# Attention with its values held stationary, and eight modulation chunks moved to the second layer's rotation and scan

## The chip, the cores and the metric

The kernel is one program on one core of a Trainium2 chip. The metric is the device time of one execution in microseconds, as a median over runs. All data is float32 except two small masks in the expert routing.

## What is computed

Two layers of a diffusion transformer over 512 tokens (256 context, 256 latent) of width 1024. Of each layer, cut to what matters here:

```python
def diff_attend(q, k, v, lam):            # 4 heads, two maps per head, 32 wide each
    s = jnp.einsum('bqhmd,bkhmd->bhmqk', q, k).astype(jnp.float32) * (DA_QK ** -0.5)
    p = jax.nn.softmax(s, axis=-1)
    a = p[:, :, 0] - lam * p[:, :, 1]
    return jnp.einsum('bhqk,bkhv->bqhv', a.astype(v.dtype), v)

for i in range(DEPTH):
    mod_x = jnp.split((c_act @ w_mod[i] + b_mod[i])[:, None, :], 6, axis=-1)   # mod_c likewise
    u = concat(ada_norm(hc, g, mod_c[0], mod_c[1]), ada_norm(hx, g, mod_x[0], mod_x[1]))
    proj = u @ w_in[i]
    o_da  = rms_norm(diff attention, subln_g) * (1.0 - lam_init)   # per head of 64 values
    o_ssd = ssd_mixer(...)                                         # a scan in chunks, both directions
    o_mla = mla_attend(...)                                        # 4 heads, 96 wide, values 64 wide
    mix = concat(o_da, o_ssd, o_mla) @ w_out[i]
    hx = hx + mod_x[2] * mix                                       # hc likewise
    hx = hx + mod_x[5] * moe_ffn(ada_norm(hx, g2, mod_x[3], mod_x[4]))   # 16 experts, top 2
return rms_norm(hx, final_norm_g)
```

Context queries see the 256 context keys, latent queries all 512. In the second layer only the latent tokens are queries.

## The kernel before

The program is written engine by engine; each engine executes its list in order and the lists meet at semaphores. A layer runs input projections, latent norms, the start and states of the scan, `rotate` (rotary embedding of queries and keys), `scan_tiles`, `attention`, `out_projection`, the router, and the experts, whose weights (about 100 MB a layer) are streamed by the SP queue.

**Attention.** A unit is one head of one kind on one tile of 128 queries. `attention_units` lists, for each tile, four "da" units (differential, two maps) and then four "ml" units: 32 units in the first layer (16 against 256 keys, then 16 against 512) and 16 units in the second (all against 512). Step s of every engine handles stages of several units:

- TensorE: scores of unit s (L737 for da, two matmuls; L740 for ml, one), transposes of the probabilities of unit s-2 (`tr`, L446), probabilities times values of unit s-3 (L770: the transposed probabilities are the stationary operand, 64 value columns the moving one).
- VectorE: maximum of the scores of unit s (L1344) and its scaling (L1345), then for unit s-1 the reciprocal of the sums and, for da, the scaling of map 1 and its subtraction (L1353 to L1356). Per group of four heads it takes the result out, squares and sums it, normalises it and places it (L1373 to L1398), with transposes by TensorE between.
- ScalarE: exponentials with row sums of unit s (L1832), copy of the transposed probabilities of unit s-2 (L1843).

Score banks alternate 2,3 and 4,5 of PSUM; the scores of unit s wait until the exponentials of unit s-2 are done.

**Modulation.** Each layer's `c @ w_mod` is 3 groups of four chunks. A chunk is a 2 MB load into one of four ring slots and one part of `spare`: 8 matmuls with tiny weights (L468). A fifth part per group transposes the row (L446, after a copy by VectorE, L1057) and places it (L1061). `spare(n)` does the next n parts wherever it is called: 5 in the first norm, 5 in `rotate` of the first layer, 7 in its `scan_tiles`, and 13 in its attention, one in each of steps 2 to 14. Then all 30 parts are done, so the calls in the second layer do nothing. SP loads the ring's chunks in the order of the list `chunks`, then writes zeros to the expert slots (25 MB), then starts on the experts; a slot is loaded again when its last reader is done.

GpSimd (POOL) works in the scan (L2028 to L2053) and is idle in the attention of before.

Of the kernel before, what the change touches and what calls it, by code (L numbers as in the profile page):

```python
# [8 lines left out]
ALU = mybir.AluOpType  # L9
# [51 lines left out]
SCAN_MODS = (1, 1, 1)  # L61
ROUTER_BANK = 5
MODS_LEFT = 13
# [3 lines left out]
LAG_OUT, LAG_NORM, LAG_TURN, LAG_PLACE = 7, 8, 9, 10  # L67
# [99 lines left out]
def head_part(s, lag):  # L167

    g, rest = divmod(s - lag, DA_H)
    return g if rest == 0 and g >= 0 else None  # L170
# [21 lines left out]
def hybrid_dit_kernel(nc, consts, x, c, ctx, c_ctx, norm_mix_g, norm_ffn_g, w_mod, b_mod, w_in, w_out, da_lambda,  # L192
# [3 lines left out]
    with ExitStack() as stack:  # L196
# [81 lines left out]
        probs_t = take(1024, tmp_at + 3072).rearrange("p (b k q) -> p b k q", b=2, q=P)  # L278
        stats = take(4 * 64, tmp_at + 4096).rearrange("p (s u m) -> p s u m", s=4, m=2)
        o_sb = take(512, tmp_at + 4352).rearrange("p (k n) -> p k n", n=256)  # L280
        o_sq = take(256, tmp_at + 4864)
# [99 lines left out]
        def turned_probs(n, nk):  # L381

            return ps[:, 6 if nk == NCTX else 6 + n % 2, :]

# [38 lines left out]
        def _(pe):  # L423
# [227 lines left out]
            def scan_tiles(l):  # L651
# [22 lines left out]
                for d in range(2):  # L674
                    cast_rows(0, d)
                    spare(SCAN_MODS[0])
                scores(1)
                cast_rows(1, 0)
                for i, t in enumerate(tiles):
# [17 lines left out]
                    if i + 1 < len(tiles):  # L697
                        cast_rows(i + 1, 1)
                        spare(SCAN_MODS[1])
                    if i + 2 < len(tiles):  # L700
                        scores(i + 2)
                        cast_rows(i + 2, 0)
                        spare(SCAN_MODS[2])
# [10 lines left out]
            def attention(l):  # L714
                units = attention_units(l)
                before, groups_before = units0 * l, units0 // DA_H * l
                pe.wait_ge(S("roped"), l + 1)
                for s in range(len(units) - DA_H + LAG_TURN + 1):
# [9 lines left out]
                    if s < len(units):  # L728
# [3 lines left out]
                        pair = 2 + 2 * (s % 2)  # L732
                        if kind == "da":
                            r0 = 64 * (hh % 2)
                            for m in range(2):
                                r = slice(r0 + 32 * m, r0 + 32 * m + 32)
                                last = nc.tensor.matmul(ps[:, pair + m, 0:nk], qk[r, hh // 2, P * t:P * t + P],  # L737
                                                        qk[r, 2 + hh // 2, 0:nk], start=True, stop=True)
                        else:
                            last = nc.tensor.matmul(ps[:, pair, 0:nk], qm[0:HD, hh, P * t:P * t + P],  # L740
# [4 lines left out]
                    if 0 <= n < len(units):  # L745
                        kind, t, hh, nk = units[n]
                        if kind == "da":
                            pe.wait_ge(S("mixed"), before // 2 + sum(1 for x in units[:n + 1] if x[0] == "da"))
                        else:
                            pe.wait_ge(S("exp_done"), before + n + 1)  # L750
                        if n >= 1 and units[n - 1][3] == NCTX:
                            pe.wait_ge(S("probs_t_ready"), before + n)
                            if nk > NCTX:
                                pe.wait_ge(S("mod_placed"), DEPTH * DEPTH_GROUPS)
# [5 lines left out]
                    n = s - 3  # L760
                    if 0 <= n < len(units):
                        kind, t, hh, nk = units[n]
                        g = n // DA_H
                        if hh == 0 and g >= 2:

                            pe.wait_ge(S("o_placed"), groups_before + g - 1)
# [7 lines left out]
                    g = head_part(s, LAG_TURN)  # L774
                    if g is not None:
                        pe.wait_ge(S("o_ready"), groups_before + g + 1)
                        for m in range(2):
                            last = tr(ps[:, g % 2, 256 + P * m:256 + P * m + P],
# [1455 lines left out]
```

## Time and profile before

| what | us |
|---|---|
| median of three runs (1418.46 to 1428.31) | 1423.97 |
| span of the profiled execution | 1417.9 |
| TensorE busy in it | 1172.4 (83%) |
| VectorE busy | 463.5 (33%) |
| ScalarE busy | 266.9 (19%) |
| GpSimd busy | 122.1 (9%) |

The span is that of one execution. In the chain of work that ended last, TensorE has 61% of the span, DMA 20%, VectorE 11% and ScalarE 3%. A float32 matmul stands as two records in the views, a transpose as one.

### The profile page before, as it was taken

How to read it: one execution, taken by the hardware profiler on the slowest of the kernel's cores; microseconds unless marked ns; L12 is line 12 of the kernel's file. 1: busy time of each engine (PE TensorE's matmuls, PEld its weight loads, DVE VectorE, ACT ScalarE, POOL GpSimd, SP SyncE). 2: the span in 40 equal slices, each digit the busy share in tenths (PEclk: the TensorE clock that was granted, in tenths of full speed). 3: DMA queues.
4: the chain of work that ended last, by engine and by line, in shares of the span. 5: the costliest groups of instructions: out<-in, count | busy, mean ns of one | idle time of the engine just before them, and what ended most of it. 6: DMA issues, size and time to landing. Idle time of an engine off the chain costs nothing.

```text
span 1417.9 us, 15930 instructions
## 1 busy us (share of the span) xinstructions
PE 1172.4 (83%) x6032; PEld 567.1 (40%) x6032; DVE 463.5 (33%) x1121; ACT 266.9 (19%) x592; POOL 122.1 (9%) x107
## 2 busy tenths in 40 slices
PE   5899978878989599999985499986799699995553
PEld 2363433444654333333332447432468333332222
DVE  5111456764742611111101421357663511110003
ACT  1220101223530411111101322001251311110002
POOL 2000031820000010000000200033200100000001
PEclk9999999979899799999998699997689799997776
DMA  9622106739996389999999401006003689999972
GB/s 337 242 86 93 60 0 261 289 131 412 374 353 274 140 326 372 389 390 395 395 399 397 187 4 56 0 0 237 0 1 119 252 313 385 388 410 413 407 327 93
DMA packets 86997, 344.03 MB, mean 243 GB/s; under 512 B 6918, under 2 KB 42187, under 8 KB 64395
## 3 DMA queue, kind: packets, MB, share of 16 engines
q1 hardware_dynamic: 67728, 309.68, 56.5%
q10 hardware_dynamic: 15195, 19.86, 4.1%
q0 software_dynamic: 4000, 13.49, 2.7%
q8 instruction: 48, 0.79, 0.2%
q14 instruction: 26, 0.21, 0.0%
HBM read 300.92 MB, written 42.07 MB: 242 GB/s over the span
## 4 chain that ended last, share of the span: by engine, by line
PE 61%; DMA 20%; DVE 11%; ACT 3%; issue 2%; SPq 1%; POOL 1%; ACTq 0%; POOLq 0%; DVEq 0%
PE ps L901 13%; PE ps L503 12%; DMA ring<-in_exp_w_up 10%; PE ps L924 6%; PE ps L791 6%; PE ps L512 5%; PE ps L446 4%; DMA ring<-in_w_mod 3%; DMA slots<-arena 2%; PE ps L468 2%; DMA arena<-in_exp_w_up 2%; PE ps L688 2%; PE ps L770 2%; PE ps L668 2%; PE ps L740 1%
## 5 line engine op out<-in xcount | busy, mean ns | idle before, releaser
L901 PE MATMUL ps<-ring,arena 128*32 128x256 f32 (+1 forms) x1344 | 197.8, 534 | 45.1 <-DMA ring<-in_exp_w_up 45.1
L503 PE MATMUL ps<-u,ring 128*128 128x512 f32 (+1 forms) x416 | 168.0, 564 | 9.5 <-ACT u L1743 4.0
L446 PE MATMUL ps<-cst,arena 128*128 128x128 f32 x558 | 110.3, 318 | 65.7 <-DVE arena L1445 33.0
L446 PEld LDWEIGHTS ps<-cst,arena 128*128 128x128 f32 x558 | 70.2, 160 | 172.0 <-issue 81.5
L901 PEld LDWEIGHTS ps<-ring,arena 128*32 128x32 f32 (+1 forms) x1344 | 71.3, 136 | 154.4 <-issue 146.5
L1601 DVE TENSOR_TENSOR arena<-arena,ps 128x128 f32<-128x128 f32 (+1 forms) x59 | 27.3, 503 | 317.3 <-ACT arena L1903 317.3
L503 PEld LDWEIGHTS ps<-u,ring 128*128 128x128 f32 x416 | 80.0, 194 | 94.9 <-issue 90.1
L901 PE MATMUL ps<-arena 128*64 128x512 f32 (+1 forms) x544 | 82.2, 528 | 17.6 <-DMA arena<-in_exp_w_up 17.6
L924 PE MATMUL ps<-arena 128*32 128x256 f32 (+1 forms) x672 | 94.4, 485 | 1.6 <-ACT arena L1912 1.6
L791 PE MATMUL ps<-u,ring 128*128 128x512 f32 (+1 forms) x256 | 83.6, 487 | 2.3 <-DVE h L1426 1.3
L512 PE MATMUL ps<-ring,u 128*128 128x256 f32 (+1 forms) x224 | 76.6, 502 | 7.7 <-DVE arena L1245 7.7
L1611 DVE COPY arena<-ps 128x512 f32<-128x512 f32 (+1 forms) x44 | 26.4, 601 | 161.6 <-DMA slots<-arena 85.7
L1903 ACT ACTIVATE arena<-ps 128x256 f32<-128x256 f32 (+1 forms) x44 | 15.3, 348 | 331.6 <-PE ps L901 302.8
L791 PEld LDWEIGHTS ps<-u,ring 128*128 128x128 f32 x256 | 48.3, 190 | 35.9 <-issue 29.7
L512 PEld LDWEIGHTS ps<-ring,u 128*128 128x128 f32 x224 | 44.3, 200 | 37.6 <-issue 34.3
L468 PE MATMUL ps<-ring,cond 128*32 128x512 f32 x384 | 52.1, 670 | 8.3 <-DMA ring<-in_w_mod 6.7
L2012 POOL DMA_INDIRECT arena<-slots,slot_ids x12 | 12.1, 1008 | 541.1 <-ACTq L1945 538.1
L1832 ACT ACTIVATE arena<-ps,arena 128x512 f32<-128x512 f32 (+1 forms) x72 | 43.9, 614 | 64.3 <-DVE arena L1345 61.8
L901 PEld LDWEIGHTS ps<-arena 128*64 128x64 f32 (+1 forms) x544 | 29.2, 133 | 63.2 <-issue 59.8
L1344 DVE TENSOR_REDUCE arena<-ps 128x2 f32<-128x1024 f32 (+3 forms) x48 | 39.5, 822 | 36.3 <-PE ps L740 29.4
L924 PEld LDWEIGHTS ps<-arena 128*32 128x32 f32 (+1 forms) x672 | 31.9, 122 | 46.5 <-issue 41.2
L770 PE MATMUL ps<-arena 128*128 128x64 f32 x320 | 46.7, 291 | 1.9 <-ACT arena L1843 1.9
(291 smaller groups left out, 1221.9 us busy)
## 6 DMA issues: line engine op xcount, KB each, us to landing
ring<-in_w_mod SPq DMA_DIRECT2D x24, 2048.0 KB, 10.9
ring<-in_exp_w_gate SPq DMA_DIRECT2D x22, 2048.0 KB, 18.6
ring<-in_exp_w_up SPq DMA_DIRECT2D x22, 2048.0 KB, 23.0
arena<-in_exp_w_down SPq DMA_DIRECT2D x22, 2048.0 KB, 20.1
slots<-zeros SPq DMA_DIRECT2D x4, 6144.0 KB, 41.9
arena<-in_exp_w_gate SPq DMA_DIRECT2D x10, 2048.0 KB, 20.7
u<-in_exp_w_down SPq DMA_DIRECT2D x10, 2048.0 KB, 19.7
arena<-in_exp_w_up SPq DMA_DIRECT2D x10, 2048.0 KB, 26.7
```

The costliest lines, as they stand in the source:

```text
L446: return nc.tensor.transpose(dst, src, ident[0:n, 0:n])
L468: last = nc.tensor.matmul(bank[32 * j:32 * j + 32, :], cond[:, k, :], w[:, k2, 512 * j:512 * j + 512], start=(k == 0), stop=(k == 7), tile ...
L503: last = nc.tensor.matmul(bank[row:row + width, 0:T - c0], w[:, k, n:n + width], u[:, k, c0:T], start=(k == 0), stop=(k == KT - 1))
L512: last = nc.tensor.matmul(bank[:, i * width:(i + 1) * width], u[:, k, P * t:P * t + P], w[:, k, n:n + width], start=(k == 0), stop=(k == K ...
L668: last = nc.tensor.matmul(ps[:, 2 + b, :], ones[:, :], ews[i % 2][d][:, 4 * b:4 * b + 4, :].rearrange("p h i -> p (h i)"), start=True, sto ...
L688: last = nc.tensor.matmul(ps[:, 4, 64 * hh:64 * hh + 64], ews[i % 2][d][:, hh, :], xdt_of(i, d)[:, 64 * hh:64 * hh + 64], start=(d == 0 an ...
L770: last = nc.tensor.matmul(ps[:, g % 2, 64 * hh:64 * hh + 64], probs_t[:, n % 2, k, :], v[:, k, 64 * hh:64 * hh + 64], start=(k == 0), stop ...
L791: last = nc.tensor.matmul(bank[:, 0:T - c0], w[:, k, P * m:P * m + P], u[:, k, c0:T], start=(k == 0), stop=(k == KT - 1))
L901: last = nc.tensor.matmul(ps[n * part:n * part + n, 2 + b % 2, 0:2 * width].rearrange("p (s n) -> p s n", s=2), x_k, pair[:, :, a:a + widt ...
L924: last = nc.tensor.matmul(ps[n * part:n * part + n, 6 + b % 2, 0:width], hid_t[:, f % 2, n * (f // 2):n * (f // 2) + n], w[:, f, width * p ...
L1344: link(v.tensor_reduce(mx[:, s, 0:nm], ps[:, pair:pair + nm, 0:nk], AX.X, ALU.max))
L1832: last = a(probs[:, s % 3, m, 0:nk], ps[:, 2 + 2 * (s % 2) + m, 0:nk], ACT.Exp, scale=DA_SCALE if kind == "da" else MLA_SCALE, bias=nb[:, ...
```

## The change

The units of a tile alternate da and ml. Each kind has score banks of its own (da 2 and 3, ml 4). The score scales go into the queries when they are copied out of PSUM, so the maximum is written negated at once and the exponential needs no scale. The ml probabilities are divided by their sum before the transposes, by GpSimd. The values become the stationary operand and the transposed probabilities (128 columns) the moving one; two heads run side by side in the columns of the array, once per two units of a kind. The result comes out with features on partitions, so it needs no transposes; the mean of squares over a head is a matmul with a block matrix of ones. The chunks of groups 1 and 2 of the second layer are loaded after its input projection chunks, and their ten parts run in its `rotate` (5) and `scan_tiles` (2, 2 and 1); the first layer's attention keeps 3 parts.

```diff
-SCAN_MODS = (1, 1, 1)
+SCAN_MODS = ((1, 1, 1), (2, 1, 0))
-MODS_LEFT = 13
+MODS_LEFT = 3
+MODS_FIRST = 20
-LAG_OUT, LAG_NORM, LAG_TURN, LAG_PLACE = 7, 8, 9, 10
+HEAD_UNITS = 2 * DA_H
+LAG_PV, LAG_SQUARE, LAG_MEAN, LAG_ROOT, LAG_ML, LAG_DA = 3, 10, 10, 11, 11, 12
...
-            for t in range(0 if layer == 0 else NCTX // P, TT) for kind in ("da", "ml") for hh in range(DA_H)]
+            for t in range(0 if layer == 0 else NCTX // P, TT) for hh in range(DA_H) for kind in ("da", "ml")]
...
-        chunks += [("mod", 1, g, k) for g in range(3) for k in range(4)]
+        chunks += [("mod", 1, 0, k) for k in range(4)]
         chunks += [("out", 0, n, 0) for n in range(2)]
-        after = [("in", 1, n, 0) for n in ("x", "bcv", "dtm", "qk", "z")] + [("out", 1, n, 0) for n in range(2)]
+        after = [("in", 1, n, 0) for n in ("x", "bcv", "dtm", "qk", "z")]
+        after += [("mod", 1, g, k) for g in (1, 2) for k in range(4)]
+        after += [("out", 1, n, 0) for n in range(2)]
```

In TensorE's attention:

```diff
-                            pe.wait_ge(S("exp_done"), before + n + 1)
+                            pe.wait_ge(S("ml_scaled"), (before + n) // 2 + 1)
...
-                        for k in range(nk // P):
-                            last = nc.tensor.matmul(ps[:, g % 2, 64 * hh:64 * hh + 64], probs_t[:, n % 2, k, :],
-                                                    v[:, k, 64 * hh:64 * hh + 64], start=(k == 0),
-                                                    stop=(k == nk // P - 1))
+                    if 0 <= n < len(units) and n % 4 >= 2:
+                        for k in range(nk // P):
+                            for unit in (n - 2, n):
+                                hh = units[unit][2]
+                                r, c = 64 * (hh % 2), P * (hh // 2)
+                                last = nc.tensor.matmul(heads_of(kind)[r:r + 64, c:c + P],
+                                                        v[:, k, 64 * hh:64 * hh + 64], probs_t[:, unit % 4, k, :],
+                                                        start=(k == 0), stop=(k == nk // P - 1),
+                                                        tile_position=(0, r))
...
+                    i = tile_part(l, s, LAG_MEAN)
+                    if i is not None:
+                        pe.wait_ge(S("o_squared"), units0 // HEAD_UNITS * l + i + 1)
+                        nc.tensor.matmul(ps[:, 5, 0:256], head_ones, o_sq, start=True,
+                                         stop=True).then_inc(S("o_means"), 1)
```

In VectorE's attention:

```diff
-                        link(v.tensor_reduce(mx[:, s, 0:nm], ps[:, pair:pair + nm, 0:nk], AX.X, ALU.max))
-                        ts(nb[:, s, 0:nm], mx[:, s, 0:nm], -(DA_SCALE if kind == "da" else MLA_SCALE), None,
-                           ALU.mult).then_inc(S("max_ready"), 1)
+                        v.tensor_reduce(nb[:, s, 0:nm], scores_of(kind)[:, :, 0:nk], AX.X, ALU.max,
+                                        negate=True).then_inc(S("max_ready"), 1)
...
-                            link(v.reciprocal(rr[:, n, 0:1], rs[:, n, 0:1]))
+                            v.reciprocal(rr[:, n, 0:1], rs[:, n, 0:1]).then_inc(S("mixed"), 1)
...
+                if kind == "da":
+                    dve.wait_ge(S("o_root"), tiles_back + i + 1)
+                    placed = stt(u[:, 0:2, P * t:P * t + P], heads, vec[:, l, V_SUBG:V_SUBG + 1],
+                                 o_root.rearrange("p (m n) -> p m n", n=P), ALU.mult, ALU.mult)
...
+                    placed = v.tensor_copy(u[:, 6:8, P * t:P * t + P], heads)
```

In ScalarE's attention:

```diff
+                        a(o_sq, heads_of("da"), ACT.Square).then_inc(S("o_squared"), 1)
+                        rsqrt(o_root, ps[:, 5, 0:256], S("o_root"), 1.0 / (DA_V * keep), small[:, 21 + l:22 + l])
```

In GpSimd's list, between the scan and the experts:

```diff
+            def attention(l):
+                for n, (kind, _, _, nk) in enumerate(attention_units(l)):
+                    if kind == "ml":
+                        pool.wait_ge(S("mixed"), units0 * l + n + 1)
+                        part = probs[:, n % 3, 0, 0:nk]
+                        g.tensor_scalar(part, part, rr[:, n, 0:1], None, ALU.mult).then_inc(S("ml_scaled"), 1)
```

TensorE in the attention of the first layer, third tile of queries, before. L737 and L740 are the scores of da and ml units, L446 with x4 the transposes of one unit's probabilities, L446 with x2 those of a group's result, L770 the product with the values of one unit.

```order
L740 MATMUL ps<-arena 128x512
L446 MATMUL ps<-cst,arena 128x128 x4
L770 MATMUL ps<-arena 128x64 x4
L737 MATMUL ps<-arena 128x512 x2
L446 MATMUL ps<-cst,arena 128x128 x4
L770 MATMUL ps<-arena 128x64 x4
L737 MATMUL ps<-arena 128x512 x2
```

The same place after the change (L759 and L762 are the scores, L469 the transposes, L795 the product with the values of two units).

```order
L762 MATMUL ps<-arena 128x512
L469 MATMUL ps<-cst,arena 128x128 x4
L795 MATMUL ps<-arena 64x128 x8
L759 MATMUL ps<-arena 128x512 x2
L469 MATMUL ps<-cst,arena 128x128 x4
L795 MATMUL ps<-arena 64x128 x8
L762 MATMUL ps<-arena 128x512
L469 MATMUL ps<-cst,arena 128x128 x4
L759 MATMUL ps<-arena 128x512 x2
L469 MATMUL ps<-cst,arena 128x128 x4
```

The two kinds alternate, and two of every four steps carry a product with values, of eight matmuls.

TensorE in `rotate` and the start of `scan_tiles` of the second layer, before (L608 and L613 rotate the ml queries and keys, L659 are the scan's scores, L668 cast decay rows, two matmuls for each tile and direction).

```order
L608 MATMUL ps<-arena,cst 96x256 x4
L613 MATMUL ps<-arena,cst 32x256
L659 MATMUL ps<-arena 128x128 x2
L668 MATMUL ps<-arena,ones 128x512 x4
L659 MATMUL ps<-arena 128x128 x2
L668 MATMUL ps<-u,ones 128x512 x2
```

After, from the last query rotation on (L631, L636, L682 and L691 are the same four lines, L491 is the modulation chunk, L469 with modrow its transposes).

```order
L631 MATMUL ps<-arena,cst 96x256
L491 MATMUL ps<-ring,cond 32x512 x8
L636 MATMUL ps<-arena,cst 32x256
L469 MATMUL ps<-cst,modrow 128x128 x4
L682 MATMUL ps<-arena 128x128 x2
L691 MATMUL ps<-arena,ones 128x512 x2
L491 MATMUL ps<-ring,cond 32x512 x16
L691 MATMUL ps<-arena,ones 128x512 x2
L491 MATMUL ps<-ring,cond 32x512 x16
L682 MATMUL ps<-arena 128x128 x2
L691 MATMUL ps<-u,ones 128x512 x2
```

One chunk stands behind each of the four query rotations, and two behind each of the scan's first two castings.

## Rows read from the trace of the kernel before

**Rows 1.** Windows: stretch, length, busy us per engine, granted clock, DMA share, GB/s.

```profile
320.00:357.00 37.00, 33.20 (x242) 15.79 (x241) 18.68 (x65) 12.87 (x46) 0.00 (x0) 0.95 1.02 410
363.00:376.00 13.00, 13.00 (x46) 9.10 (x44) 9.33 (x23) 5.10 (x13) 0.00 (x0) 0.50 1.09 385
1012.00:1042.00 30.00, 25.37 (x79) 14.80 (x77) 21.15 (x51) 10.57 (x29) 0.00 (x0) 0.50 0.00 1
```

**Rows 2.** Chain that ended last, first layer's attention: start us, length us, what.

```profile
309.14 1.03 ACT arena L1832 x4
...
311.44 3.57 PE ps L468 x16
...
330.66 1.90 PE ps L468 x16
332.57 16.18 DMA ring<-in_w_mod
...
357.41 1.17 DVE arena L1344
...
387.60 1.08 PE ps L737 x4
...
402.56 0.70 DVE arena L1344
...
409.70 2.41 PE ps L791 x5
```

**Rows 3.** The same chain, second layer's attention.

```profile
1019.33 1.23 DVE arena L1344
1020.79 1.46 ACT arena L1832 x4
...
1061.74 0.84 PE ps L770 x8
...
1063.67 0.44 PE ps L446 x4
...
1073.04 7.19 PE ps L791 x32
```

**Rows 4.** Timeline of a da unit against 512 keys: start, us, engine, line.

```profile
1056.67 0.16 DVE L1353 RECIPROCAL arena<-arena 128x2 f32<-128x2 f32 x1
1057.58 0.75 DVE L1356 SCALAR_TENSOR_TENSOR arena<-arena 128x512 f32<-128x512 f32 x1
1058.14 0.58 ACT L1843 COPY arena<-ps 128x512 f32<-128x512 f32 x1
1058.59 0.68 DVE L1344 TENSOR_REDUCE arena<-ps 128x1 f32<-128x512 f32 x1
```

**Rows 5.** Timeline of a da unit against 256 keys, VectorE.

```profile
313.21 0.16 DVE L1353 RECIPROCAL arena<-arena 128x2 f32<-128x2 f32 x1
313.98 0.48 DVE L1356 SCALAR_TENSOR_TENSOR arena<-arena 128x256 f32<-128x256 f32 x1
```

**Rows 6.** Chain, first layer's experts: 8 matmuls in two column halves, 512 columns.

```profile
523.27 3.58 PE ps L924 x16
```

**Rows 7.** Timeline, second layer: VectorE beside GpSimd, and GpSimd alone.

```profile
963.41 3.92 POOL L2035 TENSOR_TENSOR u<-cst,arena 128x1024 f32<-128x1024 f32 x2
963.48 2.10 DVE L1171 TENSOR_TENSOR arena<-arena,cst 128x256 f32<-128x256 f32 x1
...
992.40 1.04 POOL L2041 TENSOR_TENSOR arena<-arena 128x512 f32<-128x512 f32 x1
```

**Rows 8.** Timeline, TensorE in the second layer's rotation and scan.

```profile
969.47 4.88 PE L608 MATMUL ps<-arena,cst 96*96 96x256 f32 x8
...
988.86 1.95 PE L668 MATMUL ps<-u,ones 128*128 128x512 f32 x4 [1.61 <-DVE arena L1267]
990.66 1.89 PE L688 MATMUL ps<-arena 128*128 128x64 f32 x16
```

**Rows 9.** DMA of the modulation chunks, from issue to landing.

```profile
DMA to landing us min/median/max: 7.3/10.9/32.7
```

More of the change, by code:

```diff
@@ L164, in first_row, with tile_part, pairs_done, placed_count @@
     return 256 * (rank + min(rank, 8))
-def head_part(s, lag):
-    g, rest = divmod(s - lag, DA_H)
-    return g if rest == 0 and g >= 0 else None
+def tile_part(layer, s, lag):
+    i, rest = divmod(s - lag, HEAD_UNITS)
+    return i if rest == 0 and 0 <= i < len(attention_units(layer)) // HEAD_UNITS else None
+def pairs_done(n):
+    return 4 * (n // HEAD_UNITS) + 2 * (n % HEAD_UNITS // 4) + n % 2 + 1
+def placed_count(layer, i, kind):
+    return 2 * (len(attention_units(0)) // HEAD_UNITS * layer + i) + (2 if kind == "da" else 1)
 def z_after(layer, n):
@@ L675, in scan_tiles @@
                     cast_rows(0, d)
-                    spare(SCAN_MODS[0])
+                    spare(SCAN_MODS[l][0])
                 scores(1)
@@ L715, in attention @@
                 units = attention_units(l)
-                before, groups_before = units0 * l, units0 // DA_H * l
+                before = units0 * l
                 pe.wait_ge(S("roped"), l + 1)
-                for s in range(len(units) - DA_H + LAG_TURN + 1):
+                for s in range(len(units) - HEAD_UNITS + LAG_MEAN + 1):
                     if s == 1:
@@ L747, in attention @@
                         if kind == "da":
-                            pe.wait_ge(S("mixed"), before // 2 + sum(1 for x in units[:n + 1] if x[0] == "da"))
+                            pe.wait_ge(S("mixed"), before + n + 1)
                         else:
-                            pe.wait_ge(S("exp_done"), before + n + 1)
+                            pe.wait_ge(S("ml_scaled"), (before + n) // 2 + 1)
                         if n >= 1 and units[n - 1][3] == NCTX:
@@ L1333, in attention @@
                 units = attention_units(l)
-                mx, nb, rs, rr = (stats[:, s] for s in range(4))
+                nb, rs, rr = (stats[:, s] for s in range(3))
+                for a in range(2):
+                    for c in range(2):
+                        last = v.memset(head_ones[64 * a:64 * a + 64, 64 * c:64 * c + 64], float(a == c))
+                link(last)
                 lam(l)
-                for s in range(len(units) - DA_H + LAG_PLACE + 1):
+                for s in range(len(units) - HEAD_UNITS + LAG_DA + 1):
                     if s == 2:
@@ L1358, in attention @@
                         else:
-                            link(v.reciprocal(rr[:, n, 0:1], rs[:, n, 0:1]))
+                            v.reciprocal(rr[:, n, 0:1], rs[:, n, 0:1]).then_inc(S("mixed"), 1)
                     spare(mod_in_attention(l, s))
-                    for lag, part in ((LAG_OUT, take_out), (LAG_NORM, norm_out), (LAG_PLACE, place_out)):
-                        g = head_part(s, lag)
-                        if g is not None and DA_H * g < len(units):
-                            part(l, g)
@@ L1622, in _ @@
             v.memset(small[:, 20:21], EPS)
+            for l in range(DEPTH):
+                v.memset(small[:, 21 + l:22 + l], EPS / (1.0 - lam_init(l)) ** 2)
             link(v.memset(cond[:, :, :], 0.0))
@@ L2084, in _ @@
                         weights(i + 2, 0)
+                attention(l)
                 experts(l)
```

145 lines of the change are left out of this document (65 added, 80 removed).

## The prediction

> **What bounds the kernel now.** I read the windows over both attentions first, then the chain of work that ended last inside them, then the timeline of single units. Both attentions lie wholly on the chain. Units against 512 keys take 357.41 to 409.70 in the first layer, 52.3 us from the first maximum to the output projection [rows 2], and 1019.33 to 1073.04 in the second, 53.7 us [rows 3]. No one engine fills them: in 1012 to 1042 TensorE is busy 25.4 of 30 us at a granted clock of 0.50, the lower of its two levels, and VectorE 21.2 [rows 1]. Four da units in a row are paced by VectorE (two wide maxima of 1.23 and a mixing of 1.66 a unit, which is 1056.67 to 1058.33 [rows 3, 4]), while TensorE has only two score matmuls (1.08), transposes (0.44) and a product with values (0.84) [rows 2, 3]. Four ml units in a row are paced by TensorE. In the first layer's first two tiles modulation chunks stand between the units, and the chain waits 16.18 us for the last of them to land [rows 2], while DMA moves 410 GB/s [rows 1].
>
> What follows an attention hangs on its end. The output projection waits for all placed heads, and so do SP's first two expert down loads; the rest of the expert stream waits for the router. So a microsecond saved or lost at the end of an attention is one of the total. The sum below is made against the span of 1417.9. The median of the runs is 1423.97, 0.4% more, and I carry the difference over to it.
>
> **First layer, units against 256 keys.** Ten parts leave (eight chunks and two transposing parts), with the wait of 16.18. Two chunks and one transposing part stay: the first at the half clock (3.57), the second at the full one (1.90) [rows 2]. Counting on from 311.44, 3.57 + 1.90 and some 2.4 for the scores and transposes between put the maximum of unit 4 near 319.3. From there VectorE and ScalarE form a loop: mixing of a da unit 1.25 (313.21 to 314.46 [rows 5]), maximum of the next da unit 0.68 (512 elements, as the ml maximum [rows 4]), its exponentials 1.03 [rows 2], 0.1 for handing over: 3.06, and I take 3.2 for a pair. The ml unit fits into the gaps. Six pairs bring the first unit against 512 keys to 338.5. I add 1 for the ends of tiles and 2 for stretches at the half clock, where TensorE gets nearer to 4 a pair: 341.5 against 357.4, **-16** (-12.5 if all of it is at the half clock, -18 if none is).
>
> **Units against 512 keys.** The loop is now mixing 1.66, maximum 1.23, exponentials 1.46 [rows 3, 4], handing over 0.1: 4.45 a pair. In every second pair TensorE is later than that: after the exponentials come ScalarE's copy (0.58 [rows 4]), the product with values and the next scores (1.08 [rows 2]), which with 0.9 for the product is 2.6, against a mixing of 1.66. That is 0.95 more, or some 0.5 a pair; the short maximum of the other pair comes 0.3 late. I take 5.1 a pair.
>
> The new product is not in this trace. It is 8 matmuls, 16 records of 128 columns, two halves of the array at a time. The experts' L924 runs 16 records of 512 columns in two halves in 3.58 [rows 6]; a quarter of that is 0.90. If nothing ran side by side, it would cost what two products of before do, 2 x 0.84 = 1.68 [rows 3]. I take 0.90, since L924 has the same arrangement; the other end costs 0.4 a pair, 6 in all.
>
> The new scaling by GpSimd is not in the trace either. Nearest is its two-input product of the same 512 columns, 1.04 alone [rows 7]; the lower end is half of that (one input less), the upper 1.96, one of the two larger operations beside VectorE in 963.41 to 967.3 [rows 7]. I take 1.04. It begins after the reciprocal, which stands ahead of the short maximum, and ends before the exponentials of the da unit do, so it costs nothing up to about 1.3. Beyond this the transposes of the ml unit, and the scores queued behind them on TensorE, come later by the whole excess.
>
> Here a rule speaks against the change. VectorE's L1171, which has two inputs in SBUF, takes 2.10 for 256 elements beside GpSimd [rows 7]; the mixing has such an operation, which takes 0.75 for 512 with GpSimd idle [rows 4]. By my order of events GpSimd is done when the mixing starts. The Trainium skill (SBUF — State Buffer, "Who interferes with whom") says that a VectorE instruction with two SBUF inputs and a GpSimd one that reads SBUF shut each other out for a whole instruction. If each scaling met a mixing, the 16 pairs would lose up to 1.04 each, which is part of the second rival below.
>
> From the first maximum to the last are 7.5 pairs, 38.3; the drain to the output projection is 7.1 of before (402.56 to 409.70 [rows 2]), since the new chain of square, mean, root and placing is about as long as the old; 1 for a tile's end. That makes 46.4, and 1.5 for the half clock: 47.9 against 52.3, **-4.4**. In the second layer the clock is low where attention starts, from before 1012 until 1042 [rows 1]. TensorE's pair is 2 x 1.0 scores, 2 x 0.44 transposes and 0.9, 3.8 at the full clock, so 7.6 at the half one instead of 5.1. Before, 23 of the 54 us were low. I take 10 us of it after (3.5 more), because the product with values no longer waits for its stationary loads; 50.5 against 53.7 with the rest: **-3** (from -7 without half clock, to +11, the third rival).
>
> **Small edits.** Four memsets of the block matrix are short VectorE instructions (0.16 as the reciprocal [rows 4]) on the chain in each layer: **+1.2** for both, 0 to 2. Scales in the copies of queries change no instruction's size. The earlier zero writes lie beside the attention.
>
> **The moved chunks.** Eight chunks and two transposing parts enter a stretch where TensorE waits often. The first three land early, as DMA is idle; the fourth waits for the slot of the last z chunk, still ahead of its use. The first is used at about 970.7, behind the first query rotation (970.7 from 969.47 [rows 8] and one rotation at half clock), and takes 3.57. The four chunks of group 2 are queued on SP, each behind the slot of one of group 1: they start at 974.3, need 4 x 2.1 MB at 410 GB/s, 20.5, plus 2.2 (the shortest landing of 7.3 less its transfer of 5.1 [rows 9]), so the last lands at 997. TensorE's list has the chunk (1.9), two score matmuls (0.5) and a casting (1.95 [rows 8]) before the first product of the scan: 1001.3 instead of 990.66 [rows 8], **+10.7**. All that follows in the scan comes behind it (the outputs, GpSimd's weights of the next tile, and so attention). The bounds: +5 if the loads overlap better, +25 if rotation and scan run at the half clock throughout (eight chunks at 1.67 more and slower castings).
>
> **Sum.** -16 - 4.4 - 3 + 1.2 + 10.7 = -11.5: a span of 1406.4, a median of **1412**.
>
> **Rivals.** First, it goes better: the clock is full through both attentions, since dense value products take the place of weight-bound ones, and the moved chunks cost 8: -18 - 6 - 7 + 1 + 8 = -22, 1402. For it speaks that the chunks after the one at 311 take 1.90 instead of 3.57 [rows 2]; against it that 363 to 376 ran at 0.50 with TensorE busy all the time [rows 1]. Second, no gain: GpSimd needs 2.0 instead of 1.04, or meets the mixing, for 0.7 in each of 16 pairs (+11), or the moved chunks cost 10 more at the half clock: 1423. Third, slower: the half clock holds through both attentions. Then 7.5 x 7.6 + 8.1 = 65 in each, +12.8 and +11.4, with -12.4 for the short units: +23.7 in all, 1448. It decides the sign from an average pair of 5.8, that is from some 28% of the pairs at the half clock; before, 23 of 54 us were so in the second layer. Against it: the clock rose in both attentions of before.
>
> **Chances.** The forecast (1406 to 1418) 0.45, the better case 0.25, no gain 0.22, the slower case 0.06; 0.02 for anything else. Within 1% is about what a measurement of this kernel can tell from no change. Faster by over 1% means below 1409.7: the better case and a third of the forecast, 0.40. Slower by over 1% is the third rival, 0.06. The same is 0.54. The range 1398 to 1427 leaves out the slower case and the edges of the others.
>
> **What would show it.** No wait for a modulation chunk in the first attention, and its first 512-key unit near 341. Pairs of 5.1 at the full clock, with ScalarE's exponentials and VectorE's mixing back to back. GpSimd's scaling near 1 us. The scan's first product in the second layer 10 us later against the start of the rotation. I am wrong where GpSimd's scaling takes 2 us, where pairs are 7 or more, or where TensorE waits for no chunk in the second scan.

## The result, and the profile after

The changed kernel takes 1435.51 us, median of 4 runs (1434.53 to 1436.87), against 1421.28 (1418.46 to 1428.31) for the kernel before: a ratio of 1.0105, with a 95% interval of 1.0074 to 1.0137. The prediction was 1412, with 1398 to 1427 as its range, counted from 1423.97, the median of the first three runs before. It is wrong in sign. The medians and ratios leave out two executions that ran in a slower state of the chip, 1506.53 of c1 and 1791.96 of the kernel before.

The page of the changed kernel: span, and busy time of each engine.

```profile
span 1433.3 us, 15854 instructions
PE 1176.5 (82%) x6020; PEld 552.7 (39%) x6020; DVE 445.3 (31%) x1053; ACT 271.1 (19%) x598; POOL 154.4 (11%) x131
```

The span grew by 15.4 us, from 1417.9. Each profile is cut below at the same events: the first maximum of an attention, its first 1024-wide maximum, the output projection, the second layer's input projection. The column "scan" is the stretch from that projection to the second attention's first maximum, so it holds projection, rotation and scan. The last column has the mean granted clock in the three attention stages.

| kernel (run) | L0, 256 keys | L0, 512 keys | scan | L1 attention | span | clocks |
|---|---|---|---|---|---|---|
| before | 49.1 | 52.4 | 201.0 | 53.7 | 1417.9 | .90 .87 .79 |
| after | 37.9 | 58.7 | 213.7 | 62.0 | 1433.3 | .68 .77 .68 |
| a1 | 49.4 | 57.6 | 200.6 | 61.6 | 1431.8 | .90 .85 .68 |
| a2 | 36.4 | 55.6 | 213.9 | 55.7 | 1425.1 | .73 .82 .76 |
| a3 | 37.8 | 53.6 | 213.3 | 49.4 | 1415.7 | .68 .82 .80 |
| a4 | 37.8 | 53.5 | 214.3 | 49.4 | 1415.9 | .68 .82 .80 |
| b1 | 37.7 | 53.5 | 214.8 | 49.8 | 1418.1 | .68 .85 .84 |
| b2 | 37.8 | 55.0 | 213.6 | 53.2 | 1420.6 | .73 .83 .78 |
| b3 | 37.9 | 55.0 | 213.6 | 50.7 | 1419.1 | .68 .88 .91 |
| b4 | 37.4 | 54.2 | 215.4 | 49.0 | 1418.5 | .92 .81 .85 |
| c1 | 37.7 | 52.6 | 213.4 | 49.2 | 1417.8 | .73 .88 .90 |
| c2 | 39.1 | 54.3 | 204.5 | 48.7 | 1410.6 | .85 .81 .88 |
| c3 | 39.0 | 51.9 | 203.9 | 48.7 | 1408.1 | .87 .90 .96 |
| c4 | 49.3 | 52.1 | 201.3 | 51.5 | 1417.6 | .90 .90 .84 |

The short units gave 11.2 us. The 512-key units of the first layer lost 6.3, the stretch with the scan 12.7, and the second attention 8.3; what is left over, -0.7 in all, lies between the stages. Each row is one execution, and the same code can differ in it: b4 and c2 are alike up to the second layer's scan, and have 37.4 and 39.1 in the first column.

The same windows of the changed kernel, over the three attention stages (stretch, length, busy us and count for each engine, granted clock, DMA share, GB/s; they answer to [rows 1]):

```profile
308.70:346.60 37.90, 32.21 (x161) 15.50 (x162) 20.71 (x65) 17.97 (x65) 6.46 (x7) 0.68 0.84 288
346.60:405.20 58.60, 47.76 (x262) 26.60 (x262) 29.93 (x64) 29.88 (x75) 13.42 (x9) 0.77 1.02 351
1026.20:1088.20 62.00, 48.74 (x238) 27.30 (x238) 30.22 (x65) 27.80 (x70) 12.50 (x8) 0.68 0.00 1
```

TensorE works at a lower clock than before. It has less to do: its busy time times the clock, an estimate of its work, is 33.1 us in the second attention, against 36.9 before (46.71 us busy at 0.79). Who lets it stand is in the chain that ended last, second attention of the changed kernel (start us, length us, what; pieces in between are left out; it answers to [rows 3]):

```profile
1026.19 1.23 DVE arena L1374
1027.44 1.46 ACT arena L1855 x4
...
1032.92 1.58 POOL arena L2045
1035.66 2.03 PE ps L759 x4
1037.72 1.22 DVE arena L1374
1039.11 1.57 POOL arena L2045
...
1065.35 1.57 POOL arena L2045
...
1068.08 1.91 PE ps L795 x16
1069.99 2.01 PE ps L759 x4
1073.04 1.91 PE ps L795 x16
1074.95 1.81 PE ps L762 x2
```

L2045 is GpSimd's division of an ml unit, L795 the product with the values, L759 and L762 the scores. In [rows 3] no GpSimd line stood there. The instructions of L2045 by themselves, with min, median and max in ns:

```profile
L2045 POOL TENSOR_SCALAR arena<-arena x24: 922/1562/1565, 313.6 to 1079.2; 128x512 f32<-128x512 f32 x16, 128x256 f32<-128x256 f32 x8
```

So the division of 512 columns takes 1.56 us, not 1.04. What it holds up is in the timeline of one ml unit (start, us, engine, line; in brackets the idle time ahead of it and its releaser; other lines are left out):

```profile
1065.11 0.15 DVE L1392 RECIPROCAL arena<-arena 128x1 f32<-128x1 f32 x1
1065.35 1.56 POOL L2045 TENSOR_SCALAR arena<-arena 128x512 f32<-128x512 f32 x1 [4.43 <-DVE arena L1392]
1066.70 0.49 DVE L1388 TENSOR_SCALAR arena<-arena 128x512 f32<-128x512 f32 x1
1066.97 1.11 PE L469 MATMUL ps<-cst,arena 128*128 128x128 f32 x4 [1.74 <-POOL arena L2045]
1067.23 0.75 DVE L1389 SCALAR_TENSOR_TENSOR arena<-arena 128x512 f32<-128x512 f32 x1
1068.01 1.98 PE L795 MATMUL ps<-arena 128*64 128x128 f32 x16
1069.92 2.08 PE L759 MATMUL ps<-arena 32*128 32x512 f32 x4
```

TensorE stands for 1.74 us, and then transposes, product and the next scores take 1.11, 1.98 and 2.08. Where the granted clock is full, the same three take 0.66, 1.09 and 1.13. That is this stretch of the changed kernel's timeline:

```profile
364.29 0.66 PE L469 MATMUL ps<-cst,arena 128*128 128x128 f32 x4 [1.73 <-POOL arena L2045]
364.87 1.09 PE L795 MATMUL ps<-arena 128*64 128x128 f32 x16
365.90 1.13 PE L759 MATMUL ps<-arena 32*128 32x512 f32 x4
```

And in the second layer's rotation and scan, the chain (it answers to [rows 8]; L491 is a chunk, L691 a casting, L711 the scan's products):

```profile
972.91 1.90 PE ps L491 x16
974.83 16.53 DMA ring<-in_w_mod
991.40 3.43 PE ps L491 x16
995.25 1.91 PE ps L691 x4
997.17 1.73 PE ps L711 x16
```

The piece of 16.18 us that left the first attention [rows 2] stands here again, with 16.53. It isn't a stop of that length. The chain counts the load of the last chunk from the moment its ring slot came free, and TensorE works on beside it, on other chunks and a casting. How long it stands for the last chunk is in the brackets of its timeline, before and after:

```profile
348.79 3.30 PE L468 MATMUL ps<-ring,cond 128*32 128x512 f32 x16 [1.85 <-DMA ring<-in_w_mod]
```

```profile
991.40 3.43 PE L491 MATMUL ps<-ring,cond 128*32 128x512 f32 x16 [3.04 <-DMA ring<-in_w_mod]
```

With the chunks just ahead of these TensorE stood for 3.0 us in all before (1.18 and 1.85) and for 5.1 after (0.95, 1.15 and 3.04). What the chain says is that the last chunk can't begin before its load has landed.

### The profile page after: what moved, and what is told of

Its sections match the earlier page's. It is cut to its first block, busy times and chain, and to the rows that moved or that the text cites. A ratio compares the mean times of both kernels' runs of the same rounds, so it can differ in the third digit from the quotient of the medians.

```text
span 1433.3 us, 15854 instructions
## 1 busy us (share of the span) xinstructions
PE 1176.5 (82%) x6020; PEld 552.7 (39%) x6020; DVE 445.3 (31%) x1053; ACT 271.1 (19%) x598; POOL 154.4 (11%) x131
## 4 chain that ended last, share of the span: by engine, by line
PE 61%; DMA 20%; DVE 10%; ACT 3%; issue 2%; POOL 2%; SPq 1%; ACTq 0%; POOLq 0%; DVEq 0%
PE ps L926 12%; PE ps L526 12%; DMA ring<-in_exp_w_up 10%; PE ps L949 6%; PE ps L816 6%; PE ps L535 5%; PE ps L469 4%; DMA ring<-in_w_mod 3%; PE ps L491 2%; DMA slots<-arena 2%; PE ps L795 2%; DMA arena<-in_exp_w_up 2%; PE ps L711 2%; PE ps L759 1%; DVE arena L1374 1%
## 5 line engine op out<-in xcount | busy, mean ns | idle before, releaser
L469 PE MATMUL ps<-cst,arena 128*128 128x128 f32 (+1 forms) x534 | 108.8, 326 | 81.1 <-DVE arena L1453 33.0
L469 PEld LDWEIGHTS ps<-cst,arena 128*128 128x128 f32 (+1 forms) x534 | 67.1, 161 | 191.0 <-issue 81.6
L491 PE MATMUL ps<-ring,cond 128*32 128x512 f32 x384 | 54.4, 694 | 9.4 <-DMA ring<-in_w_mod 8.4
L2053 POOL TENSOR_TENSOR arena<-arena 128x512 f32<-128x512 f32 x12 | 13.3, 1130 | 332.9 <-DVE arena L1258 313.5
```

The source lines that it names most:

```text
L469: return nc.tensor.transpose(dst, src, ident[0:n, 0:n])
L491: last = nc.tensor.matmul(bank[32 * j:32 * j + 32, :], cond[:, k, :], w[:, k2, 512 * j:512 * j + 512], start=(k == 0), stop=(k == 7), tile ...
```

## The experiments

The runs whose names begin with a, b and c were measured in three groups, each with runs of the kernel before beside it. A ratio is against those, and between groups the ratios are compared.

The first four kernels take the change apart. a1_new_attention is the kernel after with the modulation chunks where they were before (parts and load order). a2_moved_chunks is the kernel before with the chunks moved as in the change, and nothing else. a3_scale_dve gives the division to VectorE:

```diff
-                            pe.wait_ge(S("ml_scaled"), (before + n) // 2 + 1)
+                            pe.wait_ge(S("mixed"), before + n + 1)
...
-                            v.reciprocal(rr[:, n, 0:1], rs[:, n, 0:1]).then_inc(S("mixed"), 1)
+                            link(v.reciprocal(rr[:, n, 0:1], rs[:, n, 0:1]))
+                            part = probs[:, n % 3, 0, 0:nk]
+                            ts(part, part, rr[:, n, 0:1], None, ALU.mult).then_inc(S("mixed"), 1)
```

a4_no_scale has the first of these two edits and no division at all.

> The new attention alone: all 13 modulation parts stay in the first layer's attention, as before the change. Theory P (attention itself is what lost): the second layer's attention takes 62 us as after the change (54 before), the first layer's units against 512 keys 59 (52 before), and with the chunk wait of 16 us back in the first layer the whole is about 15 us slower than before, 1436. Theory M (the moved chunks lost, attention is level): within 5 us of before.

Measured: 1431.98 us, ratio 1.0079 (1.0062 to 1.0097). The new attention alone is slower by 5.2 and 7.9 us in its two 512-key stages, and gives nothing in the short units, where the chunks still stand.

> The old attention with the eight chunks moved to the second layer. Theory P: the first layer's units against 256 keys are 12 to 18 us shorter, the second layer's rotation and scan 12.7 longer, so 0 to 5 us faster than before, 1416 to 1421. Theory M: 10 us slower than before or more, since the wait for the last chunk (16.5 us) is only moved and the first layer gives little back.

Measured: 1423.06 us, ratio 1.0013 (0.9997 to 1.0030). The move alone is worth nothing: -12.7 in the short units, +12.9 in the scan stretch, and +3.2 and +2.0 in the 512-key stages, whose clock fell from 0.87 and 0.79 to 0.82 and 0.76.

> The changed kernel with the ml probabilities scaled by VectorE right after the reciprocal (0.5 us) instead of by GpSimd (1.56). If GpSimd's latency is what lengthens the pairs: 0.7 to 1 us less for each of 16 pairs against 512 keys, 0.4 for the others, 12 to 18 us faster than the changed kernel, near 1420. If the half clock is what lengthens them: VectorE gets 0.5 more a pair, and the time moves by less than 4 us.

Measured: 1418.54 us, ratio 0.9982 (0.9964 to 1.0000). Against the kernel after that is 17 us less, from one instruction on another engine: 5.1 in the first layer's 512-key units and 12.6 in the second attention. VectorE's busy time there rose from 30.2 to 34.0 us, and its division takes 0.49.

> Left out: the division of the ml probabilities by their sum (the reciprocal stays). It takes the scaling away without giving it to another engine. GpSimd's latency as cause: 2 to 4 us faster than with the scaling on VectorE, 16 to 20 faster than the changed kernel. The clock as cause: within 4 us of the changed kernel, with the clock of both attentions still near 0.7.

Measured: 1417.66 us (one run). The stages are those of a3 to within 1.0 us, so a division on VectorE costs nothing that can be seen, and what the kernel after takes more than a3 belongs to GpSimd's.

Then, how does GpSimd's division cost 17 us? b1_pool_product leaves it on GpSimd and writes it as a product of two operands. b2_pool_half gives the upper half of the columns of a 512-key unit to VectorE. b3_filler leaves the division as it is and has TensorE do work that nobody needs ahead of the wait. b4_split_chunks is a3 with the chunks of group 1 back in the first attention, so that only group 2 is left in the rotation.

```diff
-                        g.tensor_scalar(part, part, rr[:, n, 0:1], None, ALU.mult).then_inc(S("ml_scaled"), 1)
+                        g.tensor_tensor(part, part, rr[:, n, 0:1].to_broadcast([P, nk]),
+                                        ALU.mult).then_inc(S("ml_scaled"), 1)
```

```diff
+                        if kind == "ml" and nk > NCTX:
+                            pe.wait_ge(S("probs_t_ready"), before + n - 1)
+                            for _ in range(2):
+                                nc.tensor.matmul(turned_probs(n, nk)[:, 0:256], ones[:, :], cst[:, C_COS:C_COS + 256],
+                                                 start=True, stop=True)
```

```diff
-SCAN_MODS = ((1, 1, 1), (2, 1, 0))
+SCAN_MODS = ((1, 1, 1), (0, 0, 0))
-MODS_LEFT = 3
-MODS_FIRST = 20
+MODS_LEFT = 8
+MODS_FIRST = 25
```

> The changed kernel, its scaling on GpSimd written as a product of two tensors with the reciprocal broadcast along the row, instead of the form with a scalar per partition. If the 1.56 us belong to that form, the product takes 1.04 as GpSimd's other products of 512 columns did, and the 16 pairs get 0.5 us shorter each or more: 8 to 13 us faster than the changed kernel, near 1425. If the operation takes 1.5 us too, nothing moves (within 2 us).

Measured: 1421.55 us, ratio 1.0019 (0.9994 to 1.0044), by the ratios 12 us below the kernel after. Its L2045, with min, median and max in ns:

```profile
L2045 POOL TENSOR_TENSOR arena<-arena x24: 613/1040/1042, 312.6 to 1065.3; 128x512 f32<-128x512 f32 x16, 128x256 f32<-128x256 f32 x8
```

The operation with two inputs takes 1.04 us, as in [rows 7], and the second attention 49.8 us, 0.4 more than with the division on VectorE. So even with the operation as long as the prediction had it, the change gains nothing.

> The changed kernel with the scaling of a 512-column unit shared: the first 256 columns by GpSimd (0.92 us as for the short units), the others by VectorE at the same time. Latency theory: 0.65 us less before each transpose, 10 to 14 us faster than the changed kernel, or nearly all of the 17 us that VectorE alone gave. If GpSimd disturbs VectorE by being busy at all, less than half of that.

Measured: 1422.91 us, ratio 1.0024 (1.0008 to 1.0040), second attention 53.2. GpSimd's instruction for 256 columns takes 1.08 where VectorE divides the other half at the same time, against 0.92 in the first layer's short units, where it divides alone (the second attention of b2, timeline):

```profile
1058.41 0.35 DVE L1398 TENSOR_SCALAR arena<-arena 128x256 f32<-128x256 f32 x1
1058.47 1.08 POOL L2051 TENSOR_SCALAR arena<-arena 128x256 f32<-128x256 f32 x1 [4.90 <-DVE arena L1394]
```

Why a wait of about the same length as in b1 leaves this stage 3.4 us longer stays open; its clock is lower, 0.78 against 0.84.

> The changed kernel with two useless matmuls of 256 columns (0.9 us at the full clock) that TensorE runs just before it waits for a scaled 512-column ml unit, 16 times. If the wait of 1.6 us costs twice, once as a wait and once by the lower clock that follows, the fill keeps the clock nearer to 1 in both attentions and the time falls by 3 to 8 us in spite of the added work. If only the wait counts, the clock rises too little to matter and the time stays or grows by up to 5 us.

Measured: 1421.59 us, ratio 1.0020 (1.0007 to 1.0033). The second attention of b3 (window, columns as above):

```profile
1022.00:1072.70 50.70, 42.53 (x270) 26.07 (x270) 30.43 (x65) 27.67 (x70) 12.50 (x8) 0.91 0.00 1
```

GpSimd is as busy as in the kernel after, 12.50 us, and the wait is still on the chain (1034.30, 1045.12, 1056.90 and 1066.40, each 1.57). TensorE has more to do, its clock is 0.91 instead of 0.68, and the stage is 11.3 us shorter. This is the run that tells the wait from the clock: of the 12.6 us that GpSimd's division cost there, 11.3 came through the clock, and 1.3 are left for the wait itself (1.5 against c1 below, which has 49.2 at nearly the same clock, 0.90, without the wait). In the first layer's 512-key units the shares are nearer to each other: of 5.1 us the added matmuls give 3.7 back, and at a clock of 0.88 the stage takes 55.0 with the wait and 52.6 without it (c1).

> Scaling on VectorE as in a3, and only group 2 of the second layer's modulation moved: four chunks behind its query rotations and none in its scan; group 1 stays in the first layer's attention. If the last chunk's wait (16.3 us) is what made the move worth nothing, it is gone here: the first layer's short units take about 41 us instead of 37.8, the second layer's rotation and scan 206 from the start of its projection instead of 213.3, and the whole is 3 to 6 us faster than a3, near 1414. If the chunks' matmuls are the cost and not the wait, it is level with a3.

Measured: 1415.30 us, ratio 0.9965 (0.9942 to 0.9988); the profiled execution took 1420.32, so its stages stand 5 us above the median. Five parts more in the first attention, four chunks and a transposing part, cost next to nothing (37.4 us, and a clock of 0.92 instead of 0.68; c2 and c3 below, with the same parts there, have 39.1 and 39.0 at 0.85 and 0.87, against 37.8 in a3). No chunk is waited for in the second layer any more, and yet the scan stretch is no shorter. Its chain shows why:

```profile
983.76 3.75 PE ps L691 x4
987.51 3.31 PE ps L711 x16
991.97 3.60 PE ps L711 x16
996.73 3.67 PE ps L691 x4
```

The same lines took 1.91 and 1.73 in the kernel after (its chain above, from 995.25), and 1.95 and 1.89 before [rows 8]. This scan runs at the lower clock level. That it has no chunks can't be the whole cause, since the kernel before has none there either and ran these lines at the full level. In b4 TensorE stood for 3.53 us ahead of the casting at 977.66, and the granted clock went from 1.00 (970 to 975) to 0.50 (980 to 1000); before, it was 1.00 from 990 to 1000. What made it rise there and not here stays open. Counted from the start of the layer's projection, b4 is 5.8 us behind the kernel before when the first casting starts, with four chunks done in the rotation, and 14.4 at the first maximum.

The last four runs ask whether the clock can be bought back, and where it is worth it. c1_filler_dve is a3 with the useless matmuls of b3. c2_split_scan_fill is b4 with useless matmuls in the second layer's scan, after three of its castings. c3_filled_all is c2 with useless matmuls in both attentions too, those of b3 and two of 512 columns ahead of the last transposes of the scan's result. c4_before_filled is the kernel before with one useless matmul of 256 columns ahead of each wait for a mixed da unit against 512 keys.

```diff
+            def fill(bank, n):
+                if bank == MOD_BANK and n:
+                    pe.wait_ge(S("mod_placed"), len(MOD_PARTS) // 5)
+                for _ in range(n):
+                    nc.tensor.matmul(ps[:, bank, :], ones[:, :], cst[:, C_COS:C_COS + 512], start=True, stop=True)
...
                     spare(SCAN_MODS[l][0])
+                    fill(MOD_BANK, 2 * l)
...
                         spare(SCAN_MODS[l][1])
+                        fill(MOD_BANK, 2 * l)
```

> The changed kernel with the division back on VectorE and, ahead of each of the 16 waits for a 512-key mixed probability tile, two matmuls of 256 columns whose result nobody reads. Theory: the clock of TensorE in the second attention costs time by itself. With the division on GpSimd these matmuls took the second attention from 62.0 to 50.7 us and its mean granted clock from 0.68 to 0.91; with the division on VectorE alone it stood at 49.4 us at 0.80. If the clock is what is left, it goes above 0.90 there and the stage to about 46 us (time about 1415, 3 below the 1418.5 of the division on VectorE alone). Rival: at 49.4 us the stage is bound by the VectorE and ScalarE chain, not by the clock; then the clock rises, the stage stays at 49 to 50, and the time at 1418 to 1420.

Measured: 1417.32 us, ratio 0.9990 (0.9971 to 1.0009). The clock of the second attention rose from 0.80 to 0.90, and the stage is 49.2 us instead of 49.4; the first layer's 512-key units gained 1.0. The rival holds: with the wait for GpSimd gone, the clock is no longer what the second attention hangs on.

> The version with six chunks in the first attention and the division on VectorE (1415.3), with two useless matmuls of 512 columns after three of the row casts of the second layer's scan. Theory: there the chunks are gone and the scan ran at 0.50 (16 products of 64 columns in 3.6 us instead of 1.9), so projection to first maximum stayed at 215.4 us although nothing waited for a DMA; with the clock kept up those products go back to 1.7 to 1.9 us, the stage falls by 5 to 8 us, to 208 to 210, and the time to about 1409. Rival: the scan is bound by VectorE, and the slow products hide beside it; the stage stays at 214 to 216 and the time at 1414 to 1417. That the useless matmuls themselves stand in the way would show as a stage above 217.

Measured: 1409.25 us, ratio 0.9922 (0.9896 to 0.9948), 6 us below b4 and 26 below the kernel after. The same place of the chain as in b4:

```profile
986.28 1.96 PE ps L697 x4
988.23 1.73 PE ps L718 x16
990.60 1.93 PE ps L718 x16
993.16 1.93 PE ps L697 x4
```

The windows over the last part of the stretch, from the first chunk to the first maximum, of b4 and then of c2:

```profile
959.40:1022.60 63.20, 51.27 (x195) 26.67 (x194) 31.96 (x88) 6.87 (x13) 14.04 (x11) 0.64 0.34 133
```

```profile
963.80:1016.30 52.50, 45.43 (x206) 22.49 (x206) 31.95 (x88) 6.87 (x13) 14.02 (x11) 0.83 0.42 160
```

More matmuls, a clock of 0.83 instead of 0.64, and 10.7 us less. The stretch from the projection on fell from 215.4 to 204.5. The whole execution gained less, 7.9 us by the spans; 1.7 of the difference is its longer first column.

> The same as the run before it, with two more places: two useless matmuls of 512 columns ahead of the last tile's transposes of the scan in each attention, and two of 256 ahead of each wait for a 512-key mixed tile. If the clock sets the time in scan and attention alike, the stages add up: second attention from 49.0 to about 46, first attention's 512-key units from 54.2 to about 51, projection to first maximum as in the run before it; time about 1403. If VectorE and ScalarE bound both attentions once the division is on VectorE, the result is that of the run before it within 2 us.

Measured: 1409.90 us, ratio 0.9940 (0.9917 to 0.9963). The attention stages run at 0.90 and 0.96, the first one gained 2.4 us in its profile and the second nothing; the median is that of c2. It is again the filling in the scan alone that paid.

> The kernel before, unchanged but for one useless matmul of 256 columns ahead of each wait for a mixed 512-key unit that follows another. It asks how much of the kernel before is the clock too: its 512-key stages took 52.4 and 53.7 us at a mean granted clock of 0.87 and 0.79. If the clock is worth there what it is worth in the changed kernel, the clock rises above 0.9 and the two stages lose 3 to 6 us together (time about 1416). If its pace is VectorE's, as the prediction read it, the time stays within 2 us of the kernel before, or the added matmuls lengthen it by 1 to 3 us.

Measured: 1417.19 us, ratio 0.9979 (0.9961 to 0.9997). The stages of the kernel before lose 0.3 and 2.2 us, at clocks of 0.90 and 0.84 instead of 0.87 and 0.79. This filling is worth 0.4% at most. The clock rose less than was expected, so what a full clock would give there isn't shown.

## Why the prediction was wrong, point by point

**The step that failed** is "I take 1.04. [...] so it costs nothing up to about 1.3. Beyond this the transposes of the ml unit, and the scores queued behind them on TensorE, come later by the whole excess." It failed in two halves. The duration was taken from an operation with two inputs in place of the one at hand; the operation with a scalar for each partition takes 1.56 us. The threshold itself was good: at 1.04 the division costs 0.4 us in the second attention (b1), at 1.56 it costs 12.6. But "by the whole excess" would be 0.26 in each of 8 pairs, 2 us. The other 10 to 11 came because TensorE, standing for 1.7 us in a pair, ran the pair at the lower clock level (b3). From one wide maximum of a da unit to the next, the changed kernel needs 5.4 us on the mean where the clock is full (367.07 to 383.30, three pairs), and 8.5 in 1063.58 to 1072.05. The prediction had 5.1 and 7.6 for these.

This step isn't all of the miss. Between the forecast of -11.5 and the +15.4 of the spans are 26.9 us. With the division at 1.04, b1's span is 1418.1: 15 of them by the spans, 12 by the ratios, go with the form of one instruction, and the rest with the terms below.

**How much at the half clock.** I took 10 us of the second attention at the lower level, "because the product with values no longer waits for its stationary loads". Of its 62.0 us some 40 were low (a mean of 0.68, where 0.50 is low). The sentence argued from a stall that was gone and did not ask after the stall that was new. The third rival had this right in kind. In its own terms the sign is decided at an average pair of 5.8; in the second attention the seven pairs from 1026.19 to 1072.05 average 6.6. Its size, +23.7, was too large, since the clock did rise in between (means of 0.77 and 0.68). TensorE's pair was put too short besides: the prediction took 0.44 for a unit's transposes, which is a piece of the chain [rows 3], where the instructions take 0.60 to 0.66 at the full clock.

**The short units: -16 was -11.2.** The chunks ahead came as counted (3.57 at 311.73, then 1.85). At the full clock the pairs are what I took, 3.2 (322.84 to 326.08). But the clock fell between 328 and 330, and from there the pairs take 5.2 to 5.5 (330.63, 336.15, 341.31, 346.56), where I had put "nearer to 4" and 2 us for all of it. The bound of -12.5, "if all of it is at the half clock", was itself too far. The modulation chunks had kept the clock up: in b4 and c2 five more parts in the same place leave the stage at 37.4 and 39.1, at 0.92 and 0.85. These were nearly free there. What the move bought is what the last group cost, whose chunks landed late (the last at 348.75 in the kernel before [rows 2]): b4 and c2 move that group alone.

**The moved chunks: +10.7 was +12.7, and the mechanism is as told.** Four loads of group 2 queued behind ring slots, and the last landed at 991.36, which is 178.8 us after the layer's projection began; the 997 of the prediction is 178.6 after it. TensorE stood for 3.04 us for it, and the chunk behind the wait took 3.43 at the half clock where 1.9 was counted, which is most of the 2 us between forecast and result. The first product of the scan stands at 997.17 against 990.66 before [rows 8], with the projection begun 5.8 us earlier. The bound of +25 for a half clock throughout did not come. But b4 shows the reverse side: with no chunk in the scan nothing waits for a load, and the scan, now at the half clock, takes 2.1 us more than in a3, where the wait still stands.

**512-key units of the first layer: -4.4 was +6.3.** b1 and a3 put them at 53.5 and 53.6, so without GpSimd's excess the term would have been +1.2. The new product takes 1.09 instead of the 0.90 taken from [rows 6], 1.98 at the half clock; and the stage now begins at the half clock, which holds from 346 to 359. With the chunks moved and the old attention (a2) it is 3.2 longer too; in a1, where chunks stand ahead of it and it begins at the full clock, it takes 57.6 instead of 58.7, and in c3, at 0.90, 51.9. In the second attention a3 has 49.4 against my 50.5, so there the new arrangement gives 4.3 us where 3 were forecast.

**Small edits: +1.2 was +0.7.** The four memsets stand on the chain with 0.14 and 0.20 in each layer.

**GpSimd beside VectorE.** The order of events was right: in the timeline above the division overlaps L1388 by 0.21 us and ends before L1389 starts. L1388 and L1389 take 0.49 and 0.75 in the 512-key units, as the same two lines did before with GpSimd idle (L1355 and L1356). The rule of the Trainium skill weighed there (SBUF — State Buffer, "Who interferes with whom") took nothing from this kernel; only b2, where VectorE's division starts just ahead of GpSimd's, shows 1.08 us instead of 0.92.

**The rivals.** "No gain" gave 1423 with GpSimd at 2.0; its condition came half true (1.56). What no rival did was join the two: a moderately slower GpSimd that turns into the half clock. Each had a chance of its own and the pair had none, and that was the case that came.

**Sum with the measured terms:** -11.2 + 6.3 + 12.7 + 8.3 - 0.7 = +15.4. With the division on VectorE, the two attention stages become 53.6 and 49.4, 17.7 less, a gain of 2.2 in all, as a3's span shows (1415.7).

## What to carry to other kernels

A wait on TensorE had two prices here, its length and the clock that it let fall; in the second attention the second was some nine times the first (11.3 and 1.3 us). So when an edit adds a short wait to each turn of a loop, or takes filling work out of one, cost the turn at both clock levels and treat the lower one as a case of its own, with a chance. Take an engine's duration only from a row of the same operation and form: the same 512 columns took GpSimd 1.04 us in one form and 1.56 in another. And work that stands on the queue of a half-idle engine may be paying for itself: look at the granted clock before moving it away.

## What was not expected of the hardware

GpSimd's product with one scalar for each partition is slower than its product of two operands: 1.56 against 1.04 us for 512 columns (two whole operands in [rows 7], the scalar repeated along the row in b1) and 0.92 against 0.61 for 256 (b1). The Trainium skill (GPSIMD Engine Reference, "4.1 Engine selection") has it the other way round, with operations of one input near line rate and those of two inputs at about half the speed of VectorE; for this form the runs do not agree (VectorE's own takes 0.49).

Useless matmuls made kernels faster: in b3 two of 256 columns ahead of each of 16 waits took 12 us off the kernel after, and in c2 those in the scan 6 us off b4, by the ratios. In c1, where TensorE no longer waited for GpSimd, the same matmuls raised the second attention's clock from 0.80 to 0.90 and were worth nothing in the whole (0.9990 against 0.9982).

The fastest kernel of the study is c2, at 1409.25 us (c3, with 1409.90, is level with it): new attention with the division on VectorE, group 1 of the chunks in the first attention, group 2 in the rotation, and the clock kept up in the scan. It is 0.8% below the kernel before.
